# Constant products in TensorE's waits during the first loads of a three-layer block

## The chip, the cores and the metric

The kernel runs on one core of a Trainium2 chip. The metric is the device time of one execution in microseconds (us); less is better. Three runs of the kernel before gave 1175.09, 1178.07 and 1179.08 us, median 1178.07.

## The reference

The input is x, 256 tokens of 1024 channels in f32, and a condition vector c of 1024. Three layers follow one another: an adaptive-norm layer with stick-breaking and sparse attention, one with differential attention, and a hybrid layer of a gated linear recurrence and a short convolution. Only the start matters here:

```python
mod = jnp.einsum('bd,ldm->lbm', jax.nn.silu(c), w_mod) + b_mod[:, None, :]
for i in range(DEPTH):
    sh_m, sc_m, g_m, sh_f, sc_f, g_f = [t[:, None, :] for t in jnp.split(mod[i], 6, axis=-1)]
    h = x * (1.0 + sc_m) + sh_m
    if i % 2 == 0:
        y = even_mixer(h, cos, sin, w_in_even[i // 2], w_out_even[i // 2])
```

`even_mixer` starts with `h @ w_in`, a product of 256 x 1024 by 1024 x 2500. Everything is f32, and the kernel keeps that accuracy: each factor is split into a high part and the rest, and three products (high x high, low x high, high x low) are summed.

## The kernel before, in words

Activations lie transposed, with 128 channels on the partitions and 256 tokens in the columns, in eight such blocks. Weights are loaded by SyncE's queue in slots of up to 1 MB into three raw buffers (`raw`). ScalarE writes a slot's high part (`whi`, line 166), VectorE the rest (`wlo`, line 187), in halves, eight of which are held at a time. A slot's raw buffer is free again when the rest of its last half is written.

`begin` (line 686) issues the small loads, then modulation chunks, x and weight slots in the order written in `k.first_loads` (line 703), where m is a chunk of `w_mod` (1 MB, 256 of its columns), x the input and w a slot. It transposes c, takes its silu, transposes the biases, lets VectorE compute the angles of the rope tables, and transposes x in 16 pieces of 128x128. `first_mod` (line 917) multiplies one of the first eight chunks: 16 small products that use 32 columns of the array each, four side by side, into bank 3 or 7. `quarter_chunk` (line 937) copies the result (`MR`), turns it with two transposes and sums it into the table `MOD`. Even chunks hold scale columns, odd ones shift columns, so chunks 0 and 1 serve step 0 of the first loop, 2 and 3 step 1, and so on.

`even` (line 1045) runs the first loop, four steps s of two channel blocks. In each step `modulated` computes h for both blocks (VectorE scales and shifts, ScalarE writes `hH`, VectorE `hL`), then `multiply` adds both blocks into six PSUM banks, 36 products of 128x256 per block, 72 per step. Bank 0 is the first of the six.

Each engine's queue is an order written out when the program is built. Every engine object keeps a clock of what it has been given, by costs in its methods (lines 143 to 225), and every semaphore mark has a time at which it is due by that clock. `turn` (line 466) looks at TensorE's clock and queues whatever is due: loads, splits, modulation chunks and the generators that do the small work. `pace` (line 480) moves TensorE's clock on in steps of 0.05 until a mark is due. So the order of all queues depends on the costs that TensorE's instructions are given. On the chip the queues wait for semaphores alone.

Of the kernel before, what the change touches and what calls it, by code (L numbers as in the profile page):

```python
# [11 lines left out]
ALU = mybir.AluOpType  # L12
# [79 lines left out]
def due(*marks):  # L92
    return max(counter.due[n] for counter, n in marks)
# [372 lines left out]
def turn(k, idle=False):  # L466


    now = k.pe.clock
    for t in list(k.tracks):  # L470
        t.go(now)
        if t.over:
            k.tracks.remove(t)
    weights_ahead(k)
    needed = k.mods_queued < k.mods_soon
    if needed and k.quiet < 3 or idle and not k.summing and (needed or k.mods_queued not in BY_VECTOR):
        k.mods.go(now)


def pace(k, when):  # L480

    for _ in range(20000):
        at = when()
        if at is not None and at <= k.pe.clock:
            return
        before = k.pe.clock
        turn(k, True)
        if k.pe.clock == before:
            k.pe.clock += 0.05
    raise RuntimeError("the queues wait for each other")  # L490


def start(k, bits, first=False):
    t = Track(bits)
    k.tracks.insert(0 if first else len(k.tracks), t)
    return t


def free(k, *banks):

    return all(k.bank[b].n == k.uses[b] for b in banks)
# [16 lines left out]
def fill(k, *banks):  # L518

    assert free(k, *banks)  # L520
    for b in banks:
        k.pe.wait_ge(k.bank[b], k.uses[b])
        k.uses[b] += 1


def fill_next(k, *banks):

    pace(k, lambda: read_out(k, *banks) if free(k, *banks) else None)
    fill(k, *banks)
# [87 lines left out]
def multiply(k, jobs, ks, x, x0, xs, x_low, first, last, fresh=False, spent=(0, 1), read=None):  # L617

    pe = k.pe
    for n, i in enumerate(ks):
        pace(k, lambda: due(x_low[x0 + i]) if x_low[x0 + i] else None)
        if fresh:
            pe.wait_ge(*x_low[x0 + i])
        xh, xl = x[0][:, x0 + i, xs], x[1][:, x0 + i, xs]
        seen = {}
        for out, slot, c, opens in jobs:  # L630
            st = step(k, slot)
            number, hi, lo = half_of(k, slot, i // st)
            new = slot not in seen and (n == 0 or i % st == 0)
            seen[slot] = number
            if new:
                pe.wait_ge(*k.high[number])
            pe.mm(out, hi[:, i % st, c], xh, first and opens and n == 0, False)
            pe.mm(out, hi[:, i % st, c], xl, False, False)
            if new:
                pe.wait_ge(*k.low[number])  # L640
            pe.mm(out, lo[:, i % st, c], xh, False, last and i == ks[-1])
            turn(k)
        if read is not None:
            read[i] = pe.inc()
        for slot, number in seen.items():
            st = step(k, slot)
            if i // st in spent and (i == ks[-1] or ks[n + 1] // st != i // st):
                k.multiplied[number] = pe.inc()
    return pe.inc()
# [33 lines left out]

def begin(k):
    pe, act, dve, pool, sp, m, D_ = k.pe, k.act, k.dve, k.pool, k.sp, k.m, k.D
    RV = m.RV
# [30 lines left out]


    fill(k, 4, 5, 6)
    c_turned = pe.wait_ge(*c_in).wait_ge(*ident_in).tr(m.ps[4][:, 0:8], RV[0:8, 0, :], ident[0:8, 0:8]).inc()
    silu = act.wait_ge(*c_turned).act(m.ST[:, 0:8], m.ps[4][:, 0:8], ACT.Silu).inc()
    k.silu_c = dve.wait_ge(*silu).copy(m.SC32, m.ST[:, 0:8].unsqueeze(2).to_broadcast([128, KD, 32])).inc()

    bm_turned = pe.wait_ge(*bm_in).tr(m.ps[5][:, 0:96], RV[0:96, 1, :], ident[0:96, 0:96]).inc()
    bm = dve.wait_ge(*bm_turned).copy(m.V[:, 0:96], m.ps[5][:, 0:96]).inc()
    dve.settle()
    for l in range(2):
        for ch in (1, 4):  # L730
# [168 lines left out]
def load_first(k):  # L899

    while k.first_loads:
        n = k.mod_loads if k.first_loads[0] == "m" else k.loads
        if k.first_loads[0] == "m" and (n < len(k.m.MW) or n % 2 in k.mod_sums):
            load_mod(k)
        elif k.first_loads[0] == "w" and (n < RAW or k.plan.last_half[n - RAW] in k.low):
            load_slot(k)
        else:
            return
        k.first_loads.pop(0)


def more_mods(k):
    if k.mod_loads < len(MODS):
        load_mod(k)


def first_mod(k, n, b):
    pe, m = k.pe, k.m
    ps = m.ps[(3, 7)[n % 2]]
    pe.wait_ge(*k.mod_loaded[n])  # L920
    if n == 0:
        pe.wait_ge(*k.silu_c)
    elif n > 1:
        pe.wait_ge(*k.mod[MODS[n - 2]])
    for i in range(2):
        for g in range(4):
            c = 2 * g + i
            pe.mm(ps[32 * g:32 * g + 32, 0:256], m.SC32[:, c, :], m.MW[b][:, 256 * c:256 * c + 256], i == 0, i == 1, pos=(0, 32 * g))
    k.mod_sums[n] = pe.inc()
    if k.first_loads:  # L930
        load_first(k)
    elif n >= FIRST_MODS - 2:
        more_mods(k)
    k.mods_queued += 1
# [91 lines left out]
def mod_columns(k, l, ch, j=0, n=8):  # L1026
    c0 = l * 48 + ch * 8 + j
    return k.m.MOD[:, c0:c0 + n]
# [4 lines left out]
def modulated(k, j):  # L1033

    act, dve, m = k.act, k.dve, k.m
    t = m.LT[:, 256 * j:256 * j + 256]
    shift = (0, 0, j // 2)
    pace(k, lambda: due(k.mod[shift]) if shift in k.mod else None)

    x = dve.wait_ge(*k.x_cols[j]).wait_ge(*k.mod[shift]).ts(t, t, mod_columns(k, 0, 1, j, 1), ALU.mult, mod_columns(k, 0, 0, j, 1), ALU.add).inc()  # L1040
    hi = act.wait_ge(*x).act(m.hH[:, j, TOK], t, ACT.Copy).inc()
    k.h_low[j] = dve.wait_ge(*hi).tt(m.hL[:, j, TOK], t, m.hH[:, j, TOK].bitcast(F32), ALU.subtract).inc()


def even(k):
    m, P = k.m, k.plan
    h = (m.hH, m.hL)

    k.rope_jobs, k.roped = [], {}
    banks = (0, 1, 2, 4, 5, 6)  # L1050
    widths = (128, 128, 128, 68) + (128,) * 8
    fill_next(k, *banks)
    y = [None] * 6
    for s in range(4):
        modulated(k, 2 * s)
        modulated(k, 2 * s + 1)
        jobs = []
        for i, w in enumerate(widths):
            bank, n, wide = banks[i // 2], i % 2, i >= 4
            at = 128 * (i - 4 * wide)  # L1060
            jobs.append((m.ps[bank][0:w, n * S:n * S + S], P.even_first[s][wide], slice(at, at + w), n == 0))
        if s < 3:
            multiply(k, jobs, (0, 1), h, 2 * s, TOK, k.h_low, s == 0, False, True)
        else:
            y[0] = y[1] = multiply(k, jobs[:4], (0, 1), h, 2 * s, TOK, k.h_low, False, True, True)
            start(k, keys(k, y[:2]))
            y[2:] = [multiply(k, jobs[4:], (0, 1), h, 2 * s, TOK, k.h_low, False, True)] * 4
    k.act.table(SET_EXP)
    k.k_, k.v, k.scored, k.chosen = {}, {}, None, None
    start(k, ropes(k, 4))  # L1070
    start(k, index(k))
    start(k, by_act(k, y[3], 4, m.QS[:, 2:4, :], 0.125, k.q, 1))
    start(k, by_dve(k, y[5], 6, m.KS[:, 2:4, :], k.k_, 1))
    start(k, by_act(k, y[2], 2, m.QS[:, 0:2, :], 0.125, k.q, 0))
    start(k, by_dve(k, y[4], 5, m.KS[:, 0:2, :], k.k_, 0))
    start(k, vectors(k, 1))
    jobs = [lambda k, lane, c=c: stick(k, lane, c) for c in range(4)] + [lambda k, lane, c=c: dsa(k, lane, c) for c in range(4)]
    for i in range(2):
        start(k, lane_of(k, i, jobs))
    rest = P.even_rest  # L1080
    start(k, by_dve(k, rows(k, 2, rest[0]), 2, m.VS[:, :, 0:256], k.v, 0))
    start(k, by_act(k, rows(k, 1, rest[1]), 1, m.VS[:, :, 256:512], 1.0, k.v, 1))
    for i, b in enumerate((0, 2)):
        k.rope_jobs.append((blocks(k, (b,), rest[2 + i], TOK), b, m.RD[:, 4 + 2 * i:6 + 2 * i, :], 0.125, 2 + i))


def by_act(k, y, b, out, scale, result, key):

    yield due(y)
    result[key] = k.act.wait_ge(*y).act(out, pair(k.m.ps[b]), ACT.Copy, scale=scale).inc(k.bank[b])  # L1090


def by_dve(k, y, b, out, result, key):

    yield due(y)
    result[key] = k.dve.wait_ge(*y).copy(out, pair(k.m.ps[b])).inc(k.bank[b])


def lane_of(k, i, jobs):

    while jobs:
        yield from jobs.pop(0)(k, i)
# [1367 lines left out]
```

## Time and profile before

| what | value |
|---|---|
| three runs | 1175.09, 1178.07, 1179.08 us |
| profiled execution | 1179.2 us, of which the span from first to last instruction is 1177.9 |
| TensorE busy | 1134.8 us, 96% of the span |
| VectorE, ScalarE busy | 846.7 us (72%), 628.0 us (53%) |
| mean granted TensorE clock | 0.987 |
| weights read | 229.56 MB, 196 GB/s over the span |

A granted clock of 1.00 is 2.4 GHz, 0.50 is 1.2 GHz. A matmul's duration in the rows has a tail of some 0.16 us in which the next one already runs, so the distance from one start to the next says more of the rate than the duration does. In the rows, `MW` (or `T`) with `SC` are the modulation chunks, `hH`, `hL`, `whi`, `wlo` the main loop, L157 are transposes.

### The profile page before, as it was taken

The page shows a single profiled execution, that of the slowest core. Times are in us where ns is not written, and L with a number is a line of the kernel's source. Part 1 is how long each engine was busy: PE and PEld are TensorE (multiplying, and loading weights), DVE is VectorE, ACT ScalarE, POOL GpSimd, SP SyncE. Part 2 cuts the span into 40 slices and gives each one's busy share as a digit, 9 for nine tenths or more (in the row PEclk, how much of TensorE's full clock was granted, in tenths as well). Part 3 has the DMA queues.
Part 4 walks back from the last instruction along what each step waited for, and adds up shares of the span by engine and source line. Part 5 has one row for each costly group of instructions (what it writes and reads, how often), then busy time and mean ns, then how long its engine had stood idle before and what let it go on. Part 6 is the DMA issues. An engine that isn't in the chain of part 4 may idle for free.

```text
span 1177.9 us, 23803 instructions
## 1 busy us (share of the span) xinstructions
PE 1134.8 (96%) x9940; PEld 1069.9 (91%) x9940; DVE 846.7 (72%) x1437; ACT 628.0 (53%) x1075; POOL 77.1 (7%) x101
## 2 busy tenths in 40 slices
PE   5999898999999999999999999999999999999998
PEld 3888578999998899898999999999999999999987
DVE  5679679897995788797557569858746667776743
ACT  3358437545443677666545445744554556555542
POOL 3000012000000200021000003500000001000000
PEclk8999899999999899999999999999999999999999
DMA  9953856898998634645665562653245554556550
GB/s 327 350 198 109 291 173 213 285 309 266 338 308 282 215 115 144 208 133 179 211 193 175 187 212 72 215 181 110 86 134 188 168 183 157 179 181 214 179 179 36
DMA packets 194683, 232.15 MB, mean 197 GB/s; under 512 B 4083, under 2 KB 169555, under 8 KB 194576
## 3 DMA queue, kind: packets, MB, share of 16 engines
q1 hardware_dynamic: 193984, 230.32, 59.1%
q8 instruction: 79, 1.29, 0.5%
q0 software_dynamic: 592, 0.31, 0.2%
q14 instruction: 28, 0.23, 0.1%
HBM read 229.56 MB, written 1.05 MB: 196 GB/s over the span
## 4 chain that ended last, share of the span: by engine, by line
PE 84%; DVE 10%; ACT 2%; issue 2%; DMA 1%; POOL 0%; SPq 0%; DVEq 0%; ACTq 0%
PE ps L154 83%; DVE wlo L187 2%; PE ps L157 2%; DVE hL L196 1%; DVE T L187 1%; ACT whi L166 1%; DVE first L187 1%; DVE LT L196 1%; DMA raw<-in_w_in_dram 1%; DVE LT L187 0%; DVE T L196 0%; DMA RV<-in_b_mod_dram 0%; DMA MW<-in_w_mod_dram 0%; DVE Fg L196 0%; DVE MR L196 0%
## 5 line engine op out<-in xcount | busy, mean ns | idle before, releaser
L187 DVE TENSOR_TENSOR wlo<-raw,whi 128x1024 fp32r<-128x1024 f32 (+1 forms) x346 | 408.4, 1202 | 162.6 <-ACT whi L166 161.0
L154 PE MATMUL ps<-hH,whi 128*128 128x256 f32 (+3 forms) x1792 | 518.4, 289 | 3.7 <-DVE hL L187 3.1
L154 PE MATMUL ps<-hH,wlo 128*128 128x256 f32 (+3 forms) x1792 | 507.5, 283 | 7.6 <-DVE wlo L187 7.6
L154 PE MATMUL ps<-hL,whi 128*128 128x256 f32 (+3 forms) x1792 | 507.2, 283 | 0.0
L166 ACT ACTIVATE whi<-raw 128x1024 fp32r<-128x1024 f32 (+1 forms) x346 | 349.2, 1032 | 198.2 <-PE ps L154 142.9
L154 PEld LDWEIGHTS ps<-hH,whi 128*128 128x128 f32 x1792 | 340.3, 190 | 15.2 <-issue 11.1
L154 PEld LDWEIGHTS ps<-hH,wlo 128*128 128x128 f32 x1792 | 340.7, 190 | 8.8 <-DVE wlo L187 8.8
L154 PEld LDWEIGHTS ps<-hL,whi 128*128 128x128 f32 x1792 | 341.0, 190 | 0.3
L154 PE MATMUL ps<-uL,whi 128*128 128x256 f32 x352 | 99.2, 282 | 0.0
L154 PE MATMUL ps<-uH,whi 128*128 128x256 f32 x352 | 99.0, 281 | 0.0
L154 PE MATMUL ps<-uH,wlo 128*128 128x256 f32 x352 | 98.4, 279 | 0.0
L154 PEld LDWEIGHTS ps<-uH,whi 128*128 128x128 f32 x352 | 66.2, 188 | 0.6 <-issue 0.6
L154 PEld LDWEIGHTS ps<-uH,wlo 128*128 128x128 f32 x352 | 66.4, 189 | 0.0
L154 PEld LDWEIGHTS ps<-uL,whi 128*128 128x128 f32 x352 | 66.1, 188 | 0.0
L166 ACT ACTIVATE LT<-ps 128x512 f32<-128x512 f32 (+5 forms) x51 | 23.9, 483 | 69.4 <-PE ps L154 56.6
L196 DVE SCALAR_TENSOR_TENSOR MR<-MW,SC,MR 128x512 f32<-128x512 f32 x70 | 54.2, 774 | 3.2
L187 POOL TENSOR_TENSOR LT<-LT 128x256 f32<-128x256 f32 x22 | 18.1, 824 | 490.8 <-ACT LT L166 388.7
L154 PE MATMUL ps<-oH,whi 128*128 128x256 f32 x128 | 38.4, 300 | 0.3 <-DVE oL L196 0.3
L154 PE MATMUL ps<-whi,u2L 128*128 128x512 f32 (+1 forms) x110 | 38.3, 348 | 0.0
L154 PE MATMUL ps<-whi,u2H 128*128 128x512 f32 (+1 forms) x110 | 38.2, 348 | 0.0
L154 PE MATMUL ps<-wlo,u2H 128*128 128x512 f32 (+1 forms) x110 | 38.1, 347 | 0.0
L166 ACT ACTIVATE LT<-T 128x256 f32<-128x256 f32 x32 | 13.0, 418 | 43.7 <-DVE T L196 43.7
(312 smaller groups left out, 1622.0 us busy)
## 6 DMA issues: line engine op xcount, KB each, us to landing
MW<-in_w_mod_dram SPq DMA_DIRECT2D x47, 1024.0 KB, 6.5
raw<-in_w_up_dram SPq DMA_DIRECT2D x44, 1024.0 KB, 5.5
raw<-in_w_in_dram SPq DMA_DIRECT2D x36, 1024.0 KB, 5.1
raw<-in_w_down_dram SPq DMA_DIRECT2D x27, 1024.0 KB, 5.3
raw<-in_w_gate_dram SPq DMA_DIRECT2D x22, 1024.0 KB, 7.3
raw<-in_w_in_odd_dram SPq DMA_DIRECT2D x12, 1024.0 KB, 6.2
raw<-in_w_in_even_dram SPq DMA_DIRECT2D x8, 1024.0 KB, 6.8
raw<-in_w_down_dram SPq DMA_DIRECT2D x8, 768.0 KB, 6.7
```

The lines of the kernel that those rows point to most:

```text
L154: return self.queued(self.e.matmul(out, lhsT, rhs, start=start, stop=stop, skip_group_check=True, **kw), length if pos is None else max(le ...
L157: return self.queued(self.e.transpose(out, in_, ident), 0.115)
L166: return self.queued(self.e.activation(out, in_, func, scale=scale, **kw), length)
L187: return self.queued(self.e.tensor_tensor(out, a, b, op), 0.07 + cols(out) / self.RATE)
L196: return self.queued(self.e.scalar_tensor_tensor(out, a, s, b, op0, op1), 0.07 + cols(out) / self.RATE + 0.06 * columns(s))
```

## The change

A helper `keep_clock(k, n)` queues n products of a constant with itself on TensorE: 128x128 ones (scaled) by 128x256, plain f32, into bank 0, where nobody reads them. Five places call it: one ahead of the transpose of c, three ahead of the transpose of the biases, five behind it, two behind chunk 0 and one behind chunk 1, and four in step 0 of the first loop between `modulated` and the products. The first waits for the constants to be written. Besides, `modulated` now waits for the scale chunk and the shift chunk, where it waited for the shift chunk alone.

```diff
+def keep_clock(k, n):
+
+    ones = k.m.ones.rearrange("p a n -> p (a n)")
+    for _ in range(n):
+        k.pe.mm(k.m.ps[0][:, 0:256], ones[:, 0:128], ones[:, 0:256], True, True)
...
     fill(k, 4, 5, 6)
+    pe.wait_ge(*k.ones_done)
+    keep_clock(k, 1)
     c_turned = pe.wait_ge(*c_in).wait_ge(*ident_in).tr(m.ps[4][:, 0:8], RV[0:8, 0, :], ident[0:8, 0:8]).inc()
...
+    keep_clock(k, 3)
     bm_turned = pe.wait_ge(*bm_in).tr(m.ps[5][:, 0:96], RV[0:96, 1, :], ident[0:96, 0:96]).inc()
     bm = dve.wait_ge(*bm_turned).copy(m.V[:, 0:96], m.ps[5][:, 0:96]).inc()
+    keep_clock(k, 5)
...
     k.mod_sums[n] = pe.inc()
+    if n < 2:
+        keep_clock(k, 2 - n)
     if k.first_loads:
         load_first(k)
...
-    shift = (0, 0, j // 2)
-    pace(k, lambda: due(k.mod[shift]) if shift in k.mod else None)
+    scale, shift = (0, 1, j // 2), (0, 0, j // 2)
+    pace(k, lambda: due(k.mod[scale], k.mod[shift]) if scale in k.mod and shift in k.mod else None)
-    x = dve.wait_ge(*k.x_cols[j]).wait_ge(*k.mod[shift]).ts(t, t, mod_columns(k, 0, 1, j, 1), ALU.mult, mod_columns(k, 0, 0, j, 1), ALU.add).inc()
+    x = dve.wait_ge(*k.x_cols[j]).wait_ge(*k.mod[scale]).wait_ge(*k.mod[shift]).ts(t, t, mod_columns(k, 0, 1, j, 1), ALU.mult, mod_columns(k, 0, 0, j, 1), ALU.add).inc()
...
         modulated(k, 2 * s + 1)
+        if s == 0:
+            keep_clock(k, 4)
```

## Rows read from the trace of the kernel before

**Rows 1.** The page: the chain that ended last, shares of the span by engine.
```profile
PE 84%; DVE 10%; ACT 2%; issue 2%; DMA 1%; POOL 0%; SPq 0%; DVEq 0%; ACTq 0%
```

**Rows 2.** The chain in order of time, 0 to 150 us: start, length, what.
```profile
14.69 0.43 DVE MR L181
15.16 2.45 PE ps L157 x20
...
20.93 0.55 DVE wlo L187
...
21.53 6.83 PE ps L154 x38
```

**Rows 3.** TensorE's timeline: start, length, line, operation, shapes, count, idle before.
```profile
6.93 0.42 PE L157 MATMUL ps<-CST,RV 96*128 96x96 f32 x1 [3.45 <-DMA RV<-in_b_mod_dram]
10.16 1.94 PE L154 MATMUL ps<-MW,SC 128*32 128x256 f32 x16 [2.81 <-DMA MW<-in_w_mod_dram]
12.72 1.72 PE L154 MATMUL ps<-MW,SC 128*32 128x256 f32 x16 [0.62 <-DMA MW<-in_w_mod_dram]
...
19.96 0.35 PE L154 MATMUL ps<-hH,whi 128*128 128x256 f32 x1 [2.36 <-DVE hL L187]
...
21.53 0.58 PE L154 MATMUL ps<-hH,wlo 128*128 128x256 f32 x1 [1.10 <-DVE wlo L187]
21.91 0.41 PE L154 MATMUL ps<-hH,whi 128*128 128x256 f32 x1
...
23.61 0.41 PE L154 MATMUL ps<-hH,wlo 128*68 128x256 f32 x1
23.96 1.94 PE L154 MATMUL ps<-MW,SC 128*32 128x256 f32 x16
25.82 0.58 PE L154 MATMUL ps<-hH,whi 128*128 128x256 f32 x1
26.20 0.42 PE L154 MATMUL ps<-hL,whi 128*128 128x256 f32 x1
...
27.70 0.30 PE L154 MATMUL ps<-hH,wlo 128*128 128x256 f32 x1
...
28.86 1.07 PE L154 MATMUL ps<-MW,SC 128*32 128x256 f32 x16
29.86 0.39 PE L154 MATMUL ps<-hH,whi 128*128 128x256 f32 x1
30.09 0.28 PE L154 MATMUL ps<-hL,whi 128*128 128x256 f32 x1
...
30.44 0.28 PE L154 MATMUL ps<-hL,whi 128*128 128x256 f32 x1
...
35.60 1.07 PE L154 MATMUL ps<-MW,SC 128*32 128x256 f32 x16
```

**Rows 4.** Stretches: length, busy time of each engine, TensorE's granted clock, DMA share, GB/s.
```profile
17.60:21.50 3.90, 0.47 (x2) 0.30 (x2) 2.72 (x10) 2.86 (x7) 0.00 (x0) 0.92 1.08 386
21.50:27.70 6.20, 6.17 (x35) 4.58 (x35) 3.28 (x4) 1.92 (x3) 0.00 (x0) 0.50 1.05 370
507.60:511.60 4.00, 3.96 (x26) 3.75 (x27) 2.57 (x6) 2.00 (x3) 0.00 (x0) 1.00 0.00 0
788.90:792.30 3.40, 3.40 (x83) 3.38 (x72) 3.30 (x6) 0.00 (x0) 0.00 (x0) 0.50 0.91 295
```

**Rows 5.** TensorE's timeline at two later waits.
```profile
507.64 1.13 PE L154 MATMUL ps<-LT,ones 128*128 128x256 f32 x4 [1.17 <-DVE LT L187]
...
787.83 0.38 PE L154 MATMUL ps<-Qg,Kg 128*32 128x32 f32 x11 [1.73 <-issue]
```

**Rows 6.** SyncE's issue of chunk 4, and its us to landing (last number).
```profile
23.66 0.47 SPq L224 DMA_DIRECT2D MW<-in_w_mod_dram  x1
...
MW<-in_w_mod_dram SPq DMA_DIRECT2D x1, 1024.0 KB, 8.4
```

**Rows 7.** ScalarE's and VectorE's timelines ahead of step 1.
```profile
29.10 1.53 ACT L166 ACTIVATE whi<-raw 128x1024 fp32r<-128x1024 f32 x2 [2.58 <-DMA raw<-in_w_in_even_dram]
...
34.35 0.42 DVE L187 TENSOR_TENSOR hL<-LT,hH 128x256 fp32r<-128x256 f32 x1 [0.48 <-ACT hH L166]
```

## The prediction

> **What bounds the kernel now.** I read the shares of the chain first: TensorE carries 84% of it [rows 1], so a microsecond that TensorE saves in a stretch where it is on the chain is a microsecond of the end, unless another engine or a load takes its place. Then the chain in order of time [rows 2]. Up to 15 us it is not TensorE: the bias load is followed by VectorE's long run for the rope tables, which ends in the copy of the first row of modulation sums (14.69). Behind it stand 20 transposes (15.16, for 2.45 us), then VectorE's and ScalarE's work on the first activations, the low half of the first weights (20.93), and from 21.53 on TensorE without a gap. So what stands ahead of 14.7 us on TensorE's queue is free, as long as it is over in time; between 17.6 and 21.5 TensorE waits; from 21.5 its own rate sets the end.
>
> TensorE's timeline shows at what rate [rows 3]. The same 16 products of a modulation chunk take 1.94 us at 10.16, 1.94 at 23.96, and 1.07 at 28.86. The 128x256 products of the main loop start 0.21 us apart from 21.91 to 23.61 and from 26.20 to 27.70 (1.70/8 and 1.50/7), and 0.117 apart from 30.09 to 30.44. The granted clock in the stretches says why: 0.50 in 21.5 to 27.7 (1.2 GHz instead of 2.4), after a stretch of 3.9 us in which TensorE was busy for 0.47 us [rows 4]. The column shows 1.00 also at 10 us, where the products ran at the slow rate: there the rows' durations are to be believed. So the clock was low at first, rose by 15 us, and fell in the wait before the first product. That low stretch is what the added products can remove.
>
> **The price of a dummy.** It is a 128x128 by 128x256 product of plain f32. The nearest row is the group of four with the same shape that starts at 507.64: 1.13 us for four, about 0.24 each with the tail of the last off [rows 5]. At half clock I take twice that, 0.48 (the main products go from 0.117 to 0.21). Lower end 0.4; upper end 0.86, which is what the kernel's own cost formula (L154: columns/600, thus 0.43) would give at half clock.
>
> **Part by part.** Sixteen dummies in five groups.
> One before the transpose of c: VectorE's constants are ready at 1.4 us (they are the first thing it does), so it ends near 2 us; the transpose waits for loads until just before 3.5 (the bias transpose at 6.93 has been idle 3.45 [rows 3]). Cost 0.
> Three before the bias transpose: 3 x 0.48 = 1.4 us in an idle time of 3.45. Cost 0; it would take 1.15 each to matter.
> Five behind it: from about 7.2, 5 x 0.48 = 2.4, to 9.6. The first chunk has landed at 10.16, after 2.81 us of idle [rows 3]. Cost 0 up to 0.58 each.
> Two after chunk 0 and one after chunk 1. Chunk 0 leaves TensorE near 12.0, chunk 1 starts at 12.72: 0.96 us against 0.7 at half clock, so chunk 1 may start up to 0.3 late. It ends near 14.4 + 0.3, one dummy brings it to 15.2; the transposes that wait for VectorE's copy start at 15.16. Cost 0 to 0.1, and 0 if the clock is already up at that point.
> Four behind the 20 transposes, before step 0 of the loop: from 17.6 to 18.7 at full clock, 19.5 at half. The next product starts at 19.96, and the one behind it waits for the weights' low half until 21.53. Cost 0. Nothing else on TensorE's queue is passed by them; only products of step 0 stand behind.
> Bank 0 is opened anew by the first real product behind them, and its readers come 40 us later, so no engine waits for them. SyncE's wait for a chunk's products is on a mark set ahead of the dummies. POOL has nothing in it.
>
> The added wait for the scale chunk: VectorE itself computed that chunk, ahead of the shift chunk. It is met when the wait for the shift is met; what it costs is one more check on the instruction, which I bound at 0 and, for four steps, at 0.1 us. Taken: 0.
>
> The written order. The dummies also move the clock by which `turn` and `pace` order the queues: 0.43 each. By line 703's order and the loader's 360 KB/us, that clock has chunk 0 down at 6.0, chunk 1 at 8.9, x at 11.8. With dummies chunk 0 is queued at 6.7, chunk 1 at 9.3, ending at 11.5, still below x. At step 0 it stands at 14.8 and comes to 16.5, while the first low half is due at 17.9. So the order behind is the same but for steps of 0.05 us of that clock, which may flip a neighbour here and there. I put 0 for it, and +/-1 us into the range.
>
> **The term that counts.** If the clock stays up through the wait, the stretch from 21.5 to 27.8 runs at the full rate [rows 3]:
> chunk 2, 1.94 to 1.07: 0.87;
> eight intervals from 21.91 to 23.61: 1.70 - 8 x 0.117 = 0.76;
> seven from 26.20 to 27.70: 1.50 - 7 x 0.117 = 0.68;
> three seams: 21.53 to 21.91 and 25.82 to 26.20 take 0.38 each against 0.23 at the full clock (29.86 to 30.09), and 23.61 to 23.96 about as much more: 0.45.
> Sum 2.76 us. Ends: 0, and 3.1 if all 6.2 us were halved.
>
> What is late next? Everything behind moves up by 2.76. Chunk 4 is multiplied at 35.60 [rows 3], then at 32.84; it was asked for at 23.66 and took 8.4 us, so it is there at 32.1 [rows 6]. The loads in that stretch run back to back, so they don't come earlier. Step 1's first product stands behind chunk 4, at 36.6 before, then at 33.9. It needs VectorE's low half of its activations, which starts at 34.35 now [rows 7]. That chain is TensorE-paced in part and load-paced in part: the weights' high half starts at 29.10, when its load lands [rows 7]; 1.0 for the first of the two, 1.7 for VectorE's two low halves, 0.9 + 0.4 to the end of the activations' low half give 33.2. Slack 0.7. So 2.76 passes to the main loop. The later waits for loads are on ScalarE, not on TensorE's chain.
>
> **A rule of the skill.** The granted clock was still 1.00 in the transposes and fell in the wait behind them [rows 4]. The Trainium skill, page "TensorE: Matmul & The Clock Gate", section "What's actually happening", says that the chip's windows of observation are not tied to the kernel's start. By that rule the place where the clock falls and rises differs from one execution to the next, and the profiled one is one draw. Each draw would lose another part of those 2.76 us, and the three runs of before do lie 4.0 us apart (1175.09 to 1179.08); no single trace shows it.
>
> **The sum** is made against the profiled execution: 1179.2 (span 1177.9 and 1.3 around it), thus 1176.4. The median of the three runs is 1178.07, 1.1 below. Against it 2.76 gives 1175.3. I take 2.4 for the 2.76, since executions that lost less have less to regain: **1175.7**.
>
> **The rivals.**
> (A) Clock held, as above: 1175.7, own range 1174.3 to 1177.0. For: the wait before 19.96 is 2.36 us, and becomes 1.2 with four dummies in front. In this trace, waits of 1.17 (at 507.64) were followed by clock 1.00, while one of 1.73 (at 787.83) was followed by 0.50 [rows 4, 5].
> (B) The clock falls all the same: two waits of 1.2 and 1.1 us stand nearly together, with two products between. Then the stretch after 21.5 runs as before. What is left is a later fall or an earlier rise in some executions, 0 to 1 us: 1177.6.
> (C) More than the sum. In executions where the clock is not yet up at 15.16, the 20 transposes on the chain run at half rate; nine dummies ahead bring the rise forward. A transpose takes 2.45/20 = 0.12 now, so up to 2.4 more on top of 2.76, if the median of before has such executions: 1173.2. Against: the profile has the clock up by then, and the gain would be seen in part of the runs only.
> (D) Slower. The dummies ahead of the chunks last longer than their cover. Place: TensorE's queue before chunk 0. From 0.58 us each it decides. At 0.86 the five end at 11.5 instead of 10.16, chunk 0 at 13.3, the two at 15.0; with chunk 1 and the last dummy at full clock the transposes start at 16.5 instead of 15.16 (+1.3), at half clock at 17.7 (+2.5). Between the two, +1.8, and with the clock not held nothing returns it: 1179.9. Against: the group at 507.64 has 0.24 to 0.28 each at full clock [rows 5]. A flipped order that opens a stall is of this size too.
>
> **Chances.** A 0.45, B 0.32, C 0.13, D 0.10. A measurement of this kernel tells 0.3% from no change, 3.5 us. Of C nearly all is beyond that (0.12), of A a quarter, where runs and order help (0.12): faster 0.24. Slower: of D the larger half and little else, 0.07. The rest, 0.69, is within. The range reaches to C's value on one side and past B on the other: 1173.0 to 1179.3.
>
> **What would show it.** In the profile after: granted clock 1.00 in 17.6 to 27.7; chunk 2 in 1.07 us; the main products 0.117 apart from the first; chunk 0 still at about 10.2 and the first transposes at 15.2; step 1 near 33.9 behind chunk 4 with no wait on a load; behind that the same sequence about 2.8 us earlier. B is shown by 0.50 behind 21 us; D by transposes later than 15.2; C by a larger shift ahead of 21 us. I am wrong in kind if the shift at 36 us is there and the end doesn't show it, which would be the written order, or a load that becomes late.

## The result

| | before | changed | ratio, 95% interval |
|---|---|---|---|
| median, first five runs each | 1178.07 us | 1169.97 us | 0.9932 [0.9909, 0.9955] |
| median, on another chip | 1177.59 us | 1169.79 us | 0.9940 [0.9916, 0.9963] |
| profiled execution | 1179.2 us | 1173.66 us | |

The change makes the kernel 0.6 to 0.7% faster, some 8 us; forecast were 1175.7 and a range down to 1173.0. The intervals are clear of 1. The profiled execution of the changed kernel is the slowest of its five, so the trace holds 5.5 of the 8 us.

The page of the changed kernel first: the shares of the chain (answers to [rows 1]).

```profile
span 1172.3 us, 23867 instructions
...
PE 85%; DVE 8%; ACT 2%; DMA 2%; issue 2%; POOL 0%; SPq 0%; DVEq 0%; ACTq 0%
PE ps L154 84%; DVE wlo L187 2%; PE ps L157 2%; DMA XR<-in_x_dram 1%; DVE T L187 1%; DVE hL L196 1%; ACT whi L166 1%; DVE first L187 1%; DMA raw<-in_w_up_dram 1%; DMA raw<-in_w_in_even_dram 0%; DVE LT L196 0%; DVE Fg L196 0%; ACT LT L166 0%; POOL T L187 0%; DVE LT L187 0%
```

The load of x now stands on the chain where the rope tables stood. TensorE's timeline of the changed kernel (start, length, operation, count, idle before), against [rows 3]:

```profile
3.42 2.93 PE L154 MATMUL ps<-ones 128*128 128x256 f32 x6
...
6.30 3.45 PE L154 MATMUL ps<-ones 128*128 128x256 f32 x10
10.54 1.07 PE L154 MATMUL ps<-MW,SC 128*32 128x256 f32 x16 [0.78 <-DMA MW<-in_w_mod_dram]
...
15.72 2.00 PE L157 MATMUL ps<-CST,XR 128*128 128x128 f32 x16 [0.83 <-DMA XR<-in_x_dram]
17.56 0.60 PE L157 MATMUL ps<-CST,MR 128*128 128x128 f32 x4
18.53 1.99 PE L154 MATMUL ps<-ones 128*128 128x256 f32 x8 [0.37 <-ACT LT L166]
20.89 0.39 PE L154 MATMUL ps<-hH,whi 128*128 128x256 f32 x1 [0.36 <-DVE hL L187]
21.11 0.28 PE L154 MATMUL ps<-hL,whi 128*128 128x256 f32 x1
21.23 0.28 PE L154 MATMUL ps<-hH,wlo 128*128 128x256 f32 x1
...
22.50 1.07 PE L154 MATMUL ps<-MW,SC 128*32 128x256 f32 x16
```

Here `ones` are the dummies, the constant products of the change. Four things are to be seen. Chunk 0 takes 1.07 us where it took 1.94: the clock is up by 10.5 us. A dummy is two matmuls in the records, each with a weight load of its own (6 for three, 10 for five, 8 for four). The wait of 1.10 us for the first low half of the weights, at 21.53 before, is gone, though no dummy could remove it. And all four transposes of the sums stand behind those of x, where two stood ahead of them: the order of the queue has changed. The stretches (length, busy times, granted clock, DMA), against [rows 4]:

```profile
17.60:21.50 3.90, 3.17 (x19) 2.37 (x17) 2.27 (x8) 2.06 (x5) 0.00 (x0) 1.00 1.07 386
21.50:27.70 6.20, 6.20 (x66) 4.64 (x65) 4.08 (x6) 3.06 (x5) 0.00 (x0) 1.00 0.94 317
```

The clock is held, as forecast. Lined up instruction by instruction, TensorE is 2.62 us earlier at the first product of step 1, and still about 2.5 at 762 us. Then, at 788, another 3.0 come at one place: the bursts of small products below are 2.54 apart between the two kernels, and the fourth (793.96 and 788.41) is 5.55 apart. It is the wait that [rows 5] shows only as a gap of 1.73 us. Before it, in the kernel before, stands this (TensorE's timeline):

```profile
783.99 0.90 PE L154 MATMUL ps<-Qg,Kg 128*32 128x32 f32 x72
784.82 0.39 PE L154 MATMUL ps<-hH,whi 128*128 128x260 f32 x1
...
785.38 0.73 PE L154 MATMUL ps<-Qg,Kg 128*32 128x32 f32 x61
```

and at the same work in the changed kernel

```profile
781.45 0.91 PE L154 MATMUL ps<-Qg,Kg 128*32 128x32 f32 x72
782.28 0.39 PE L154 MATMUL ps<-hH,whi 128*128 128x260 f32 x1
...
782.84 0.91 PE L154 MATMUL ps<-Qg,Kg 128*32 128x32 f32 x72
```

A burst of 72 small products was cut behind the 61st, the other 11 came 1.73 us later with nothing waited for, and the clock fell behind it [rows 4]. In the changed kernel the burst is whole.

So three parts were to be told apart: the clock at the start, the order of the queues, and this wait with the slow clock behind it.

### The profile page after: what moved, and what is told of

Same layout as the page of the kernel before. It is cut to its first block, busy times and chain, and to the rows that moved or that the text cites. A ratio compares the mean times of both kernels' runs of the same rounds, so it can differ in the third digit from the quotient of the medians.

```text
span 1172.3 us, 23867 instructions
## 1 busy us (share of the span) xinstructions
PE 1140.2 (97%) x9972; PEld 1073.9 (92%) x9972; DVE 845.9 (72%) x1437; ACT 628.0 (54%) x1075; POOL 77.5 (7%) x101
## 4 chain that ended last, share of the span: by engine, by line
PE 85%; DVE 8%; ACT 2%; DMA 2%; issue 2%; POOL 0%; SPq 0%; DVEq 0%; ACTq 0%
PE ps L154 84%; DVE wlo L187 2%; PE ps L157 2%; DMA XR<-in_x_dram 1%; DVE T L187 1%; DVE hL L196 1%; ACT whi L166 1%; DVE first L187 1%; DMA raw<-in_w_up_dram 1%; DMA raw<-in_w_in_even_dram 0%; DVE LT L196 0%; DVE Fg L196 0%; ACT LT L166 0%; POOL T L187 0%; DVE LT L187 0%
```

## The experiments

Each was timed beside before on its chip, in 4 to 12 runs of its own. There were three chips, so kernels are compared with one another by their ratios to before (after_again, narrow16, shift64 and shift256 shared one chip; full_oldplan, after192, start12 and loop4 another; low_first, shift128 and held a third). "Narrow" means that a dummy is cut to 32x32 by 32x32, which leaves the number of instructions and takes nearly all of its work away. "Old order" means that TensorE's clock in the written order isn't moved by it, nor by the wait for the constants. "Instructions added" counts TensorE's against before. Every kernel here, those in the old order too, keeps the added wait for the scale chunk; no run takes it out by itself. held and after192 carry their narrow products beside the full ones.

```diff
 narrow:
-        k.pe.mm(k.m.ps[0][:, 0:256], ones[:, 0:128], ones[:, 0:256], True, True)
+        was = k.pe.clock
+        k.pe.mm(k.m.ps[0][0:32, 0:32], ones[:, 0:32], ones[:, 0:32], True, True, pos=(0, 0))
+        k.pe.clock = was + 256 / 600.0 + 0.003      # new order
+        k.pe.clock = was                            # old order instead
```

| kernel | dummies | order | instructions added | median us | ratio to before, interval |
|---|---|---|---|---|---|
| after_again | full | new | 64 | 1169.79 | 0.9940 [0.9916, 0.9963] |
| narrow16 | narrow | new | 64 | 1171.45 | 0.9951 [0.9931, 0.9970] |
| shift64 | narrow | old | 64 | 1174.13 | 0.9980 [0.9962, 0.9999] |
| shift256 | narrow x4 | old | 256 | 1176.34 | 0.9995 [0.9975, 1.0016] |
| full_oldplan | full | old | 64 | 1172.32 | 0.9961 [0.9946, 0.9977] |
| after192 | full, 48 narrow | new | 256 | 1173.63 | 0.9963 [0.9950, 0.9977] |
| start12 | 12 full, 4 narrow | new | 64 | 1170.22 | 0.9946 [0.9929, 0.9963] |
| loop4 | 12 narrow, 4 full | new | 64 | 1170.42 | 0.9943 [0.9928, 0.9958] |
| low_first | narrow | old, one moved | 64 | 1169.78 | 0.9934 [0.9911, 0.9957] |
| shift128 | narrow x2 | old | 128 | 1174.62 | 0.9971 [0.9953, 0.9989] |
| held | full, 22 later | new | 320 | 1166.27 | 0.9899 [0.9870, 0.9928] |

**The changed kernel again.** after_again. Expected:

> The changed kernel once more, on the chip of the other three. Three parts are asked of it. (1) Clock held through the first wait: worth 2.6 us at 36 us, in every execution. (2) The wait of 1.73 us in the middle of a burst of small products at 787.8, and the slow clock behind it, which the profile after lacks: worth 2.9. (3) What is left of the 8.1 between the medians, 2.6. If (2) belongs to the program and not to chance, the median is again 7 to 9 us below before. If it was chance, the median is 3 to 5 below.

It is 0.9940: the 8 us belong to the program.

**The dummies made narrow, in both orders.** narrow16 and shift64. Expected:

> The changed kernel with its sixteen products cut to 32x32 by 32x32: as many instructions in the same places, the same written order of all queues, but hardly any work in the array. If the clock held at the start is all of the gain, it goes back to before (1178, within 1 us), with granted clock 0.50 near 21 us again. If the instruction count is behind the missing wait at 788, the start loses 2.6 as before, but the wait near 788 is not there: 1174 to 1176 and a gain of 2.5 to 5.

> The same sixteen narrow products in before's written order (they are given no cost in it), so before plus 64 instructions on TensorE (each plain f32 product is two weight loads and two matmuls). Theory of the instruction fetch: the wait near 788 is gone, 2.5 to 5 us faster than before. Theory of the written order: as before, within 1 us, and the wait is there.

With nearly no work in the array 0.0049 of the 0.0060 stays. By the medians the forecast's only term, the clock, is thus the smallest part; and the old order gives 0.9980 against 0.9951. The expectation for narrow16 had put all that isn't clock on the fetch, and missed the order: it came out at 1171.45, below both of its ranges. That the two are two orders shows in the queues that the programs write out: shift64's are before's on every engine but for the dummies, and narrow16's are the changed kernel's.

**The edge of a page of instructions.** The idea: TensorE's instructions come in blocks (pages), and a burst of small products can reach a page's end before the next page is there. shift256, shift128 and after192 move that edge, the first two being shift64 with

```diff
-    for _ in range(n):
+    for _ in range(4 * n):      # shift128: 2 * n
```

Expected:

> Four times as many narrow products, in before's written order: 256 instructions more on TensorE than before. If the wait near 788 is the fetch of the next page of 256 instructions arriving late in a burst, a shift by a whole page puts the page's edge at the same product, 61 of 72, and the wait of about 1.7 us is back: time as before within 1.5 us. If any shift removes it, or the array's small work at the start does, it is 2.5 to 5 us faster, like the kernel with 64 more.

> Two narrow products in each place of one, before's order: 128 instructions more than before. By the fetch theory the page's edge leaves the second burst (it was behind product 61, and 64 pairs earlier is the end of the first burst) and the next edge, 128 pairs on, lies in the third burst, near product 50 of 72, after 128 pairs used up in some 2.3 us: a wait of 1 to 1.7 us there, time near before's, 1175 to 1177. If any shift but a whole page helps, it is as with 64: 1174.

> The changed kernel with 48 narrow products behind its own dummies, without cost in the order: 256 instructions more than before in all. Fetch theory: the wait of 1.5 to 1.8 us after product 61 of 72 is back, so that this is 1.5 to 3.5 us slower than the changed kernel (1169.8): 1171.3 to 1173.3. If the wait near 788 had been the order's or the clock's doing, it stays away and the time is the changed kernel's.

TensorE's timelines: shift256,

```profile
781.22 0.73 PE L154 MATMUL ps<-Qg,Kg 128*32 128x32 f32 x61
783.43 0.38 PE L154 MATMUL ps<-Qg,Kg 128*32 128x32 f32 x11 [1.48 <-issue]
```

after192,

```profile
782.07 0.73 PE L154 MATMUL ps<-Qg,Kg 128*32 128x32 f32 x61
784.74 0.38 PE L154 MATMUL ps<-Qg,Kg 128*32 128x32 f32 x11 [1.94 <-issue]
```

and shift128.

```profile
786.21 0.90 PE L154 MATMUL ps<-Qg,Kg 128*32 128x32 f32 x72
...
787.65 0.59 PE L154 MATMUL ps<-Qg,Kg 128*32 128x16 f32 x49
789.33 0.45 PE L154 MATMUL ps<-Qg,Kg 128*32 128x16 f32 x23 [1.08 <-issue]
```

With 256 instructions more the cut is back behind the 61st product, in both orders, with full and with narrow dummies. With 128 more it is behind the 49th of the third burst, where product 50 was expected; with 64 more no wait over 0.3 us is put down to issue on TensorE. None of the eight profiles with 64 more, nor that of held with 320 (64 and 256), has such a wait there. So the place goes by the count of instructions, with a period of 256.

What is waited for is seen in part. The page of a profile counts the packets of a queue named instruction, in before

```profile
q8 instruction: 79, 1.29, 0.5%
```

and in shift256.

```profile
q8 instruction: 80, 1.31, 0.5%
```

A packet has 16.3 KB, and the three kernels with 256 or more instructions more on TensorE (shift256, after192, held) have one packet more than the other ten. Asked for in windows of 0.1 us, this queue has a packet at 785.2 in before, 780.9 in shift256, 782.4 in after192 and 786.9 in shift128, each 2.3 to 2.6 us ahead of the product that ends the wait. That the wait is for such a block fits all of this, but it is argued, not shown: which instructions a packet holds the traces don't say. The Trainium skill, page "Runtime: NRT & Kernel Launch", section "Instruction fetch mechanics", says that each engine's instructions are refilled in blocks of 256; by that the period is the page of instructions, and the traces agree with it. The same section of the Trainium skill calls the cost of crossing such a block's edge mostly hidden; here it shows as 1.1 to 1.9 us, in bursts in which 128 small products with their weight loads are issued in some 2 us.

Its price: shift64 against shift256 0.0015, after192 against the changed kernel 0.0023 (or 0.0031 by its first ratio), thus 2 to 4 us, though the intervals in the table overlap. The wait itself is 1.5 to 1.9; in the profiles of before and after192 the clock also fell to 0.50 behind it, in those of shift256 and shift128 not.

The runs' mean granted clocks make it sharper. Within each kernel an execution whose mean clock is 0.001 higher is 0.86 us shorter (one line through all runs of all kernels). Taken to the same clock of 0.990 by that, an estimate, the means are: before 1176.6 to 1176.9 on its three chips, shift256 1176.5 and after192 1176.3, which have the wait; shift64 1174.5, shift128 1174.8, and the changed kernel 1173.1 and 1173.4. Each is good to about 1 us (95%). So at one clock the wait is worth 2.0 us in the old order and 2.9 to 3.2 in the new one. Open is shift128: its profile has a wait of 1.08 us, yet at one clock it is only 0.3 us above shift64, and its median of 1174.62 lies just under the range expected.

**The clock alone.** full_oldplan has full dummies in the old order. Expected:

> The sixteen products at their full size, but given no cost in the written order, so every queue stands as in before. Against the kernel with the narrow ones in the same order (1174.1) this shows the clock alone. Theory of the clock: 0.50 near 21 us is gone, and 2 to 2.8 us come off: 1171.5 to 1172. Theory of the order (narrow products in the new order gave 1171.5, 2.7 less than in the old one): the clock is of little worth and this stays at 1173.5 to 1174.5, with the wait of 1.1 us for the first low half still there.

0.9961 against 0.9980 for its narrow partner, 2.2 us, though the intervals overlap and the chips differ. The trace is sharper. Its stretches,

```profile
17.60:21.50 3.90, 2.47 (x13) 1.82 (x11) 2.45 (x9) 2.83 (x6) 0.00 (x0) 1.00 1.08 387
21.50:27.70 6.20, 5.90 (x61) 4.41 (x62) 3.98 (x8) 2.20 (x4) 0.00 (x0) 1.00 1.01 354
```

and its timeline:

```profile
15.68 1.95 PE L157 MATMUL ps<-CST,XR 128*128 128x128 f32 x16
...
21.80 0.39 PE L154 MATMUL ps<-hH,wlo 128*128 128x256 f32 x1 [1.14 <-DVE wlo L187]
```

The wait for the low half is still there, 1.14 us, so the order did remove it. The transposes of x start 0.24 later than before, at 27.7 us the same product is 2.48 earlier: 2.72 us between the two, forecast 2.76.

The narrow partner's timeline (shift64) shows something more:

```profile
15.26 2.96 PE L157 MATMUL ps<-CST,XR 128*128 128x128 f32 x16
...
22.39 0.58 PE L154 MATMUL ps<-hH,wlo 128*128 128x256 f32 x1 [1.12 <-DVE wlo L187]
```

Here the 16 transposes take 2.96 us instead of 1.94, in low_first's profile 2.92 and in shift128's 3.62; in narrow16's and shift256's they take 2.00 and 1.98. That is the ratio of chunk 0's 1.94 to 1.07, so I read it as a clock that wasn't up in time (the column shows 1.00 there, as it does under the slow chunk 0 in before: the durations are to be believed). In such executions 1.0 to 1.7 us are lost on the chain. That is rival C's mechanism, at up to 1.7 of its 2.4 us; whether executions of before other than the profiled one have it, no trace shows.

**Which of the dummies.** Expected:

> The changed kernel with the four products of step 0 made narrow, the twelve ahead of it full: same order, same count of instructions. If the four hold the clock through the wait before step 0, the clock falls near 21 us here and the time is that of all narrow (1171.5). If the twelve do it, it is the changed kernel's (1169.8).

> The complement: only the four of step 0 are full, the twelve at the start are narrow. If the four are what counts, 0.50 does not appear between 17 and 28 us and the time is the changed kernel's, 1169.8 within 1 us. If the twelve are needed (they bring the clock up sooner, which the four only keep), it is 1171.5.

Both are at the changed kernel's time within what is measured, and both profiles show 1.00 in 17.6 to 27.7. In start12 it stays up through a wait of 1.92 us, as long as the one in narrow16 behind which it fell. Either group held it in the one execution profiled; that one of them is needed, or only the other, isn't borne out.

**The order.** low_first is shift64 with one instruction moved in the program:

```diff
+    if j == 0:
+        split_low(k)
     x = dve.wait_ge(*k.x_cols[j]).wait_ge(*k.mod[scale])...
```

> The narrow products in before's order (1174.1), with one instruction moved: VectorE writes the low half of the first weights before it scales the first activations, not behind them, as the changed kernel's order has it. If this is the order's share, the wait of 1.1 us for that half is gone and most of the 2.7 between the two narrow kernels comes: 1171.3 to 1173. If the share lies in the transposes that moved behind those of x, or in chance, it stays at 1174.

VectorE's timeline in low_first,

```profile
19.81 0.63 DVE L187 TENSOR_TENSOR wlo<-raw,whi 128x452 fp32r<-128x452 f32 x1 [0.30 <-ACT whi L166]
20.36 0.41 DVE L193 TENSOR_SCALAR LT<-LT,MOD 128x256 f32<-128x256 f32 x1
```

where before has it behind two rounds of LT and hL:

```profile
20.51 0.43 DVE L187 TENSOR_TENSOR hL<-LT,hH 128x256 fp32r<-128x256 f32 x1 [0.48 <-ACT hH L166]
20.85 3.50 DVE L187 TENSOR_TENSOR wlo<-raw,whi 128x452 fp32r<-128x452 f32 x4
```

Since the written clock decides all that follows, this one move shifts the small work of chunks 2 and 3 too, and low_first's queues are then in the changed kernel's order in all but the two early transposes and the sums read from them. So what low_first gains doesn't need those two moved.

0.9934 against 0.9980, with narrow dummies; 1169.78 is below the range expected. The direct part is small: the wait of 1.1 goes, but the first product comes 0.5 later in narrow16 (20.46, in before 19.96) and 1.1 later in low_first (21.73, in shift64 20.62), so the first product with the low half is 0.5 and 0.1 earlier. What comes with it is in the stretches of narrow16,

```profile
20.50:23.80 3.30, 3.30 (x20) 2.75 (x24) 2.29 (x4) 2.78 (x4) 0.00 (x0) 0.50 1.08 385
23.90:27.70 3.80, 3.80 (x50) 2.76 (x42) 1.50 (x3) 0.58 (x1) 0.00 (x0) 1.00 0.89 302
```

and of shift64.

```profile
20.90:27.70 6.80, 5.68 (x33) 3.79 (x33) 4.27 (x6) 3.36 (x5) 0.00 (x0) 0.50 0.95 330
```

With the second wait gone TensorE works on without a gap from its first product, and in the two profiles of this order with narrow dummies the clock is back after 3.4 us, in the four of the old order (before, shift64, shift256, shift128) after 6.8. That the dummies' own gain and the order's overlap follows: the order returns about half of what the clock costs, so the dummies find less to hold.

How much is there by 40 us is read from one group of products that all kernels have, a modulation chunk at 39.11 us in before:

```profile
39.11 1.07 PE L154 MATMUL ps<-T,SC 128*32 128x256 f32 x16
```

With narrow dummies it is at 39.20, 39.54 and 40.76 in the old order (shift256, shift64, shift128) and at 37.00 and 37.94 in the new one (narrow16, low_first). With full dummies it is at 36.60 in the old order and between 35.36 and 37.15 in the six profiles of the new one with full dummies in at least one group, 36.33 in the mean. So in the traces the order is worth 1.2 to 2.1 us against before where the clock falls, and about 0.3 where the dummies hold it, less than these profiles differ among themselves. The rest of low_first's 0.0046 isn't in its first 40 us; how much of it is chance stays open, and its interval overlaps narrow16's.

**The sum.** Along one path from before to the changed kernel, each step by one difference: count of instructions 0.0020 (shift64), order 0.0029 (narrow16), clock 0.0011 (after_again), together 0.0060, 7 us. By the other path, in the old order first, the clock is worth 0.0019 (full_oldplan) and the order 0.0021. Each difference is about as large as its uncertainty of 0.002; that all three are there is shown by the traces, their exact shares are not. The traces split the profiled pair's 5.5 us otherwise: 2.5 at the start, where clock and order overlap and full dummies in the old order give nearly all of it, and 3.0 at the wait, of which 1.73 is the wait and the rest the slow clock behind it. The 2.5 us that the medians hold beyond this profiled pair are not assigned.

**Later waits held too.** held adds

```diff
+def keep_later(k, n, b):
+
+    ones, was = k.m.ones.rearrange("p a n -> p (a n)"), k.pe.clock
+    assert free(k, b)
+    k.pe.wait_ge(k.bank[b], k.uses[b])
+    for _ in range(n):
+        k.pe.mm(k.m.ps[b][:, 0:256], ones[:, 0:128], ones[:, 0:256], True, True)
+    k.pe.clock = was
```

at four places. Expected:

> The changed kernel, with 22 more dummies at full size in four later waits before which the clock fell in the profiles: eight in the one of 4.5 us at 124, five in each of those of 2.8 us at 200 and 532, four in the one of 2.2 us at 377; they take no cost in the order. 42 narrow products at the start keep the edge of the page where the changed kernel has it. If the spread of the changed kernel from one execution to the next (1166.8 to 1173.7) is these falls, all of it goes: granted clock 0.998 or more, 1163 to 1166, and little spread. If the falls come anyway or the dummies end late, 1168 to 1170.

1166.27, mean granted clock 0.999 to 1.000 in its four runs; the stretches around the four waits:

```profile
117.00:127.00 10.00, 9.50 (x60) 5.97 (x60) 8.33 (x14) 6.53 (x15) 0.00 (x0) 1.00 0.98 332
195.00:205.00 10.00, 8.16 (x67) 7.76 (x66) 9.77 (x17) 9.51 (x16) 6.14 (x8) 1.00 0.52 170
370.00:382.00 12.00, 10.79 (x71) 7.30 (x71) 6.76 (x19) 3.70 (x9) 0.00 (x0) 1.00 0.77 273
520.00:530.00 10.00, 9.20 (x79) 9.00 (x77) 9.62 (x20) 8.35 (x16) 6.56 (x8) 1.00 0.61 201
```

It is 1.0% under before, and 0.4% under the changed kernel by the ratios, though these intervals overlap a little (0.9870 to 0.9928, and 0.9916 to 0.9963). The falls are gone as expected; the median lies just above the range of 1163 to 1166, and the spread did not become small. The spread of the changed kernel goes with the clock: its first five runs are 1173.66, 1169.97, 1170.01, 1168.97 and 1167.65 us at 0.991, 0.993, 0.993, 0.994 and 0.997. In held the spread (1165.15 to 1169.22) is not the clock's.

## Why the prediction was wrong

**The term that counts: right.** The clock was held, chunk 2 takes 1.07 us, and the stretch to 28 us gained 2.72 of the forecast 2.76 in the old order. No load became late, and at 762 us nothing had been given back. Step 1 started at 33.99 behind chunk 4, forecast 33.9, but that is partly luck:

```profile
32.56 1.07 PE L154 MATMUL ps<-MW,SC 128*32 128x256 f32 x16
33.99 0.39 PE L154 MATMUL ps<-hH,whi 128*128 128x256 f32 x1 [0.36 <-DVE hL L187]
```

Chunk 4 was 3.04 earlier (35.60 before), and 0.4 of it went into a wait for VectorE's low half, whose slack of 0.7 was too large. The mechanism held, then, but by the medians this term is a fifth to a third of what the kernel gained (0.0011 to 0.0019 of 0.0060), and by the profiled pair 2.5 of 5.5 us. The sum stopped there, and two terms were missing in it.

**The written order: put at 0, wrong.** The step "So the order behind is the same but for steps of 0.05 us of that clock" failed. I compared the end of chunk 1 (11.5) with x (11.8), and the four dummies of step 0 with the first low half (16.5 and 17.9), and both comparisons hold. What I left out is the small work between. By the costs from which the programs are written (read off while they are built, no run shows them) VectorE's copy of chunk 0's sums is due at 11.49 in before, ahead of the end of the pace for x at 11.84; with the dummies it is due at 12.51, behind it. That put two transposes behind x's sixteen, and chunk 0's sums behind chunk 1's. The pace for them then ends later, and the first low half, which is queued once its high half (15.02) is at most 0.1 ahead of TensorE's clock, passes that mark with the clock at 14.92 where it missed it at 14.82: so it went ahead of the first activations. Also wrong is "VectorE itself computed that chunk, ahead of the shift chunk": in the changed kernel's queue the shift chunk comes first, and the added wait is for the chunk that comes last. By the ratios the order is worth 0.0029 (narrow16 against shift64) to 0.0046 (low_first) with narrow dummies and 0.0021 with full ones (after_again against full_oldplan); the traces show 1.2 to 2.1 us and about 0.3. I had put 0 for it and 1 us into the range.

**Instruction count: not in the sum at all, and the step that cost most.** The row at 787.83 stood among my rows as the nearest wait after which the clock fell, with "issue" as its releaser. I used it for the clock and didn't ask why TensorE waited for nothing in the middle of a burst. 64 more instructions moved the edge out of it: 3.0 us in the profiled pair, 2 to 3 by the runs taken to one clock. With the 2.76 that makes 5.8, which against the median of 1178.07 gives 1172.3, still 2.3 above what was measured. It is the opposite of rival D: instructions can gain by their count.

**The price of a dummy: wrong by two.** The "x4" at 507.64 are four matmul records and two products. A plain f32 product took 0.43 us at the full clock (eight records last 1.99 us and four 1.13, thus 0.215 each) and 0.9 at half (three in 2.72, from 3.42 to 6.14), which is a little over the upper end of 0.86 that I had given to rival D. It cost nothing: the five ended 0.78 us before chunk 0 could start, the clock was up by then, and x's load set the start of the transposes.

**The rivals.** B didn't come: the seven profiles with full dummies in either group show 1.00 in that stretch. C's mechanism exists (1.0 to 1.7 us in three narrow profiles), but is not what made the time: making the dummies full gave 0.0011 and 0.0019 in all, C's part included. D didn't come. The chance of 0.24 for more than 0.3% was too low because all its cases were about the clock; the range was drawn from one mechanism's bounds.

## What to carry to other kernels

Added instructions had three effects here beside their time: what they do to the clock, what their cost does to an order that is planned by costs, and where they put the edges of the instruction pages. To know which one paid, vary one at a time: the same count with no work, the same work with no cost in the plan, and a count shifted by 256. And a wait whose releaser is "issue" in the middle of a burst of small matmuls is a candidate for the page's edge: a few instructions ahead of it may be worth as much as the change itself, here 2 to 3 us of 8.

## What the runs showed of the hardware

The instruction stream of TensorE waited 1.1 to 1.9 us at an edge if about 128 pairs of small weight loads and matmuls were issued in some 2 us ahead of it (61 of 72, 49 of 72), and not measurably with the edge 32 pairs earlier (no issue wait over 0.3 us in the profiles with 64 more). The instruction queue moved one packet of 16.3 KB more for 256 instructions more. A 128x256 plain f32 product is two matmul records 0.215 us apart at 2.4 GHz and 0.45 at 1.2. The mean granted clock of an execution ranges from 0.986 to 0.996 in before, and its time from 1181.0 to 1171.9 us, 0.86 us for each 0.001; a kernel with its long TensorE waits filled ran at 0.999 to 1.000.
